# The second layer's norm gain moves into its weights: POOL scales the weight blocks, ACT applies the row factor

## The reference, cut to what matters

```python
for l in range(DEPTH):                      # DEPTH = 2
    h = rms_norm(x, pre_norm_g[l])          # y = x * rsqrt(mean(x*x) + EPS);  y * g
    proj = einsum('bsd,de->bse', h, w_in)   # w_in_ab in layer 0, w_in_c in layer 1
    ...                                     # mixers A and B (layer 0), C (layer 1), gates
    y = einsum('bse,ed->bsd', y, w_out)
    x = x + rms_norm(y, post_norm_g[l])
```

## Time and profile before

| | us |
|---|---|
| three executions | 1218.23, 1218.73, 1219.78 |
| the profiled execution | 1218.22 |
| its span | 1216.4 |
| TensorE busy (PE) | 1186.4 |
| DVE busy | 805.5 |
| ACT busy | 589.1 |
| POOL busy | 432.4 |

### The profile page before, as it was taken

One profiled execution on the slowest core, in us unless ns is written; L12 is line 12 of the kernel. 1 busy time (PEld: TensorE's weight loads), 2 busy tenths in 40 slices (PEclk: granted clock), 3 DMA queues, 4 the chain that ended last, 5 costly groups with the idle time before them and its releaser, 6 DMA issues.

```text
span 1216.4 us, 17708 instructions
## 1 busy us (share of the span) xinstructions
PE 1186.4 (98%) x6520; PEld 1011.3 (83%) x6520; DVE 805.5 (66%) x1710; ACT 589.1 (48%) x1296; POOL 432.4 (36%) x557
## 2 busy tenths in 40 slices
PE   9999999999999999898999999999999999999995
PEld 8988888888888887787788888888888888888874
DVE  5464765756667668867554866857658568485677
ACT  6554444434444556655454544544435444345464
POOL 5433214133163464646752214124141241222312
PEclk9999999999999999999999999999999999999998
DMA  6261101011031153235121102011020110201107
GB/s 200 71 188 47 59 18 52 19 52 35 19 87 53 53 156 105 70 114 156 65 78 51 50 19 74 18 57 53 18 74 19 57 53 19 73 19 31 44 20 136
DMA packets 93560, 78.42 MB, mean 64 GB/s; under 512 B 3074, under 2 KB 83970, under 8 KB 93475
## 3 DMA queue, kind: packets, MB, share of 16 engines
q1 hardware_dynamic: 92466, 73.63, 19.9%
q0 software_dynamic: 1008, 3.67, 1.8%
HBM read 68.85 MB, written 13.68 MB: 68 GB/s over the span
## 4 chain that ended last, share of the span: by engine, by line
PE 47%; DVE 2%; ACT 1%; POOL 1%; issue 1%; DVEq 0%; ACTq 0%; POOLq 0%
PE dense L1126 26%; PE dense L1137 7%; PE pv_ps L1259 6%; PE scores L1339 4%; PE turned L1306 4%; PE turned L1294 0%; DVE pT_lo L1844 0%; DVE fin L2040 0%; POOL w_lo L978 0%; ACT k_hh L1448 0%; DVE e_sb L1779 0%; POOL rowstat L1004 0%; POOL rowstat L1001 0%; DVE y L1763 0%; ACT junk L1630 0%
## 5 line engine op out<-in xcount | busy, mean ns | idle before, releaser
L1126 PE MATMUL dense<-hT_hi,w_hi 128*128 128x512 f32 x880 | 350.7, 399 | 0.0
L1126 PE MATMUL dense<-hT_lo,w_hi 128*128 128x512 f32 x880 | 344.7, 392 | 0.0
L1126 PE MATMUL dense<-hT_hi,w_lo 128*128 128x512 f32 x880 | 344.2, 391 | 0.0
L971 POOL TENSOR_SCALAR w_hi<-w_f 128x1024 fp32r<-128x1024 f32 x86 | 93.2, 1084 | 642.2 <-PE dense L1126 585.2
L978 POOL TENSOR_TENSOR w_lo<-w_f,w_hi 128x256 fp32r<-128x256 f32 x344 | 266.3, 806 | 7.2
L1455 ACT ACTIVATE e_sb<-e_sb,low 128x256 f32<-128x256 f32 (+7 forms) x256 | 170.3, 665 | 171.5 <-DVE low L1779 169.2
L1488 ACT ACTIVATE pT_hi<-turned 128x640 fp32r<-128x640 f32 (+3 forms) x224 | 117.2, 523 | 165.7 <-PE pv_ps L1259 95.2
L1126 PEld LDWEIGHTS dense<-hT_hi,w_lo 128*128 128x128 f32 x880 | 165.5, 188 | 36.8
L1126 PEld LDWEIGHTS dense<-hT_hi,w_hi 128*128 128x128 f32 x880 | 166.0, 189 | 26.1 <-issue 0.3
L1126 PEld LDWEIGHTS dense<-hT_lo,w_hi 128*128 128x128 f32 x880 | 166.2, 189 | 25.1
L1844 DVE TENSOR_TENSOR pT_lo<-turned,pT_hi 128x640 fp32r<-128x640 f32 (+3 forms) x224 | 133.6, 597 | 39.6 <-ACT pT_hi L1488 39.4
(11 more groups left out here) (213 smaller groups left out, 1804.4 us busy)
## 6 DMA issues: line engine op xcount, KB each, us to landing
w_f<-in_w_in_c SPq DMA_DIRECT2D x37, 512.0 KB, 4.2
w_f<-in_w_in_ab SPq DMA_DIRECT2D x34, 512.0 KB, 3.9
rel_tiles_dram<-rel_rows_dram SPq DMA_DIRECT2D x1, 5120.0 KB, 23.0
bias<-rel_tiles_dram SPq DMA_DIRECT2D x8, 640.0 KB, 5.4
y<-in_x SPq DMA_DIRECT2D x8, 512.0 KB, 7.7
hT_lo_f<-in_x SPq DMA_DIRECT2D x8, 512.0 KB, 7.3
out_x<-y SPq DMA_DIRECT2D x8, 512.0 KB, 3.6
w_f<-in_w_out_c SPq DMA_DIRECT2D x8, 512.0 KB, 3.8
```

The lines of the kernel that those rows point to most:

```text
L971: ts(hi, src, 1.0, 1.0, ALU.mult, ALU.mult).then_inc(w_hi_done, 1)
L1126: last = mm(dense[:, x.n % 2, :], lhs[:, d * P:(d + 1) * P], rhs[:, d, x.f * HALF:(x.f + 1) * HALF], start=i == 0, stop=i == 23)
```

## The change

The helper `takes_g` names 37 of the weight blocks: all of layer C's input projection. For these, POOL's `split` first waits for g_pre, multiplies each of the block's eight 128x128 tiles in place by a factor per partition (a column of g_pre), waits for these to be done, and then splits as before. SP loads g_pre's eight columns with eight small loads in place of one. The instruction that applied the row's root and g_pre on DVE is removed, and ACT applies the root alone, as a copy with a scale, behind the squares of its step.

```diff
+def takes_g(w):
+    return w.u.kind == "C" and w.b != "o"
...
-                sp.dma_start(g_pre[:], pre_norm_g[1].partition_broadcast(P)).then_inc(s_gpre, 16)
+                for d in range(DT):
+                    sp.dma_start(g_pre[:, d:d + 1], pre_norm_g[1][d * P:(d + 1) * P].rearrange("(p a) -> p a", a=1))\
+                        .then_inc(s_gpre, 16)
...
-        def split(n, hi_slot, slot, loads):
+        def split(n, hi_slot, slot, loads, scaled=0):
             if new(w_loaded[slot], 16 * loads):
                 pool.wait_ge(w_loaded[slot], 16 * loads)
-            src, hi = f32_place(slot), hi_place(hi_slot)
+            src, hi, lo = f32_place(slot), hi_place(hi_slot), lo_place(slot)
+            if scaled:
+                if new(s_gpre, 16 * DT):
+                    pool.wait_ge(s_gpre, 16 * DT)
+                for d in range(DT):
+                    part = (slice(None), d // 4, slice(d % 4 * P, (d % 4 + 1) * P))
+                    last = ts(src[part], src[part], g_pre[:, d:d + 1], None, ALU.mult)
+                last.then_inc(w_scaled, 1)
+                if new(w_scaled, scaled):
+                    pool.wait_ge(w_scaled, scaled)
             ts(hi, src, 1.0, 1.0, ALU.mult, ALU.mult).then_inc(w_hi_done, 1)
...
             for w in SPLITS_AT.get(s, []):
                 freed_by(w.hi_free)
-                split(PRO_SPLITS + w.n, w.hi, w.slot, w.loads)
+                split(PRO_SPLITS + w.n, w.hi, w.slot, w.loads,
+                      1 + sum(1 for o in WEIGHTS if o.n < w.n and takes_g(o)) if takes_g(w) else 0)
...
+            for n in NORM:
+                r = n.r
+                if s == n.scaled:
+                    if new(n_xr, r + 1):
+                        act.wait_ge(n_xr, r + 1)
+                    if new(n_sum, r + 1):
+                        act.wait_ge(n_sum, r + 1)
+                    copy(x_place(r), by_tile(y[:, r, :]), ACT.Copy, scale=rowstat[:, 5, r:r + 1]).then_inc(n_scaled, 1)
...
-            for n in NORM:
-                r = n.r
-                if s == n.scaled:
-                    if new(n_xr, r + 1):
-                        dve.wait_ge(n_xr, r + 1)
-                    if new(s_gpre, 16):
-                        dve.wait_ge(s_gpre, 16)
-                    if new(n_sum, r + 1):
-                        dve.wait_ge(n_sum, r + 1)
-                    stt(out=x_place(r), in0=by_tile(y[:, r, :]), scalar=rowstat[:, 5, r:r + 1], in1=by_tile(g_pre[:]),
-                        op0=ALU.mult, op1=ALU.mult).then_inc(n_scaled, 1)
```

More of the change, by code:

```diff
@@ L719, in program @@
     w_loaded = [sem(f"w_loaded{i}") for i in range(7)]
-    w_hi_done, w_ready = sem("w_hi_done"), sem("w_ready")
+    w_scaled, w_hi_done, w_ready = sem("w_scaled"), sem("w_hi_done"), sem("w_ready")
     s_filled, s_hi_out = sem("filled"), sem("hi_out")
@@ L973, in split @@
                 pool.wait_ge(w_hi_done, n + 1)
-            lo = lo_place(slot)
             for h in range(2):
```

## The result

| | before | after |
|---|---|---|
| median of the executions | 1218.48 (4) | 1267.20 (4), from 1266.44 to 1267.88 |
| ratio after / before | | 1.0398, 95% interval 1.038 to 1.0416 |
| the profiled execution, its span | 1218.22, 1216.4 | 1267.12, 1265.3 |
| mean granted clock of TensorE | 0.995 | 0.979 |

The median before now has a fourth execution, 1217.97. The forecast was 1218.3 in a range from 1216.2 to 1222.4. The change costs 4.0%, and the time lies far above the range.

What follows compares the result with a forecast made beforehand. TensorE, busy 98%, bounds the kernel; only its 9.4 us of waits for normalisation between the layers could be won. First rows -1.0 plus bridge +0.6 gave -0.4, a median of 1218.3 us, range 1216.2 to 1222.4.

Steps and rivals of the forecast that it cites:

- Part 1: Rows 0 to 3, normalised while units of kind B run: DVE relieved; -1.0 us, between 0 and -2.0.
- The price of a multiplication: POOL's added 128x128 multiplication by g_pre: 0.30 us each, 2.5 us per block, between 2.0 and 3.7.
- In the long stage of C ... nothing: Layer C's long stage: 2.5 us per split lie beside two fills, so they cost nothing.
- Part 2: Rows 4 to 7, bridge into layer C: 2.8 us won turn into waits; +0.6 us, between -0.6 and +3.
- The wait for v of C1: Bridge: the split of v ends at 584.95, TensorE gets there at 582.4 and must wait 2.5 us.
- (a): Bridge: scaled splits k, g, v end about 564.0, row 4's root behind them; its sum some 0.25 us late.
- the +0.6 of the sum: Bridge: TensorE turns row 6 at 586.95 where before it did at 586.35, +0.6 us.
- (d): Splits from 593 on, each waiting for TensorE to free the high part: slack 2.8 us against 2.5, barely holds.
- the dear rival: POOL's multiplications cost 0.45 us each, 3.7 per block, over the slack: +6.4, 1225; decides from 0.36 each; chance 0.20.
- The rule weighed: POOL and DVE contend for SBUF at 577 to 584 us; applying this would move the sum by 0.2.
- The clock: TensorE's new bridge waits, up to 3.9 us, lower its clock: 1.6 us lost, sum +1.2, 1220; chance 0.2.
- DVE was the only cause: Roots not delayed, multiplications cost 0.25: bridge -0.6, first rows -2.0, time 1216.1; chance 0.10.

Runs made afterwards that it cites:

- Experiment 8: Changed kernel, but DVE instead of ACT applies the row factor, as a one-input operation; POOL's scaling stays: 1268.14 us, ratio 1.0408.
- experiment 5: Changed kernel with constant 1.0 in place of g_pre in POOL's eight multiplications per block, product with g_pre left out: 1227.48 us, ratio 1.0072.
- experiment 2: Changed kernel with only four of each scaled block's eight tiles multiplied, the other half left out: 1229.92 us, ratio 1.0081.
- experiment 3: Changed kernel with the output weights' split ahead of the scaled split of v in five units of layer C: 1236.71 us, ratio 1.0141.
- experiment 1: Changed kernel with no block scaled, layer 1's product with g_pre left out, row factor still on ACT: 1215.83 us, ratio 0.997.
- experiments 6: Changed kernel with one wide two-input multiplication per block, g_pre's eight columns broadcast, in place of eight small ones: 1223.11 us, ratio 1.004.
- experiment 7: Changed kernel with one wide two-input multiplication per block, done before POOL waits for the free high part: 1222.07 us, ratio 1.0026.
- experiments 9: Kernel of experiment 7 with the block v of unit C1 multiplied by itself earlier, ahead of the bridge's roots: 1218.65 us, ratio 0.9999.
- 13: Kernel of experiment 9 with the row factor of rows 0 to 3 on DVE, rows 4 to 7 on ACT: 1218.57 us, ratio 1.0.
- 14: Kernel of experiment 13 with the output weights' split ahead of that of v in five units of layer C: 1218.22 us, ratio 0.9996.

## Why the prediction was wrong

By its own steps:

**Part 1 was right.** Forecast -1.0, measured -1.1 (508.88 to 507.75); the matmul behind the first wait stands 1.4 us sooner, as said (486.82 to 485.43). The 2.6 us wait at the first rows is down to 1.2, and the clock of 486.8 to 491 is 1.00 where it was 0.61. Experiment 8 adds that ACT is not needed for it: a shorter instruction on DVE wins 1.6. Why that is 0.5 more was not tested by itself; of the waits, the one for the factor itself is 1.3 us with ACT and 0.6 with DVE.

**The price of a multiplication failed: the first wrong step.** "I take 0.30 each, as the shape is the mask's", 2.5 per block, 3.7 at most. Measured: 0.60 median, 4.67 per block. The mask carries its factors in the instruction, the new form reads one per partition from SBUF, and experiment 5 shows that this is all of the difference. I had written that no row showed the form, and then set the upper bound by a guess (what doubling the columns costs) rather than by a row. A safe upper bound near by would have been the two-input operation, 0.71 us for 128x256, or 5.7 for eight.

**"In the long stage of C ... nothing" failed: the second wrong step.** 31.5 of the 48.9 us arise at its five places. I had read the slack only of the blocks that are scaled. The unscaled one behind v on POOL had 0.18 us, and 0.53 of idle time ahead of it. The two errors work on each other, so neither is the whole: at the assumed price (experiment 2) the time is 37.3 us less and this step still costs 8.2 us of waits; by order alone, at the true price (experiment 3), it is 30.5 us less. The 540 us window at 538.3 busy was read as "nothing to win", which is true; it says nothing about how near to losing each of its waits is.

**Part 2, the bridge: the right places, the sizes too small, mostly by the price.** The wait for v of C1 came, behind its split as described, and row 6 behind that; the forecast was 2.5 us for the wait and 586.95 for row 6, measured were 4.65 and 596.20. In (a) three scaled splits were to end at 564.0. They end at 570.71, 6.7 us late, and 3 x (4.75 - 2.5) = 6.75 says why (4.75 with the wait ahead of the split, as in the 2.5). That alone brought a wait of 5.94 us. With the assumed price, experiment 2, the wait at v of C1 was 2.4, but row 6 was turned 1.6 us late for the +0.6 of the sum, and 2.8 us of clock came on top, which the sum left to a rival. (d) failed as the dear rival said: 4.75 against 2.8 of slack, and a wait of 1.79.

**The rule weighed.** The Trainium skill, "GPSIMD Engine Reference", section "Engine selection", calls a one-input operation on GpSimd roughly line rate. Experiment 5 and the added form differ by a factor of two at one shape, so no single rate holds for one-input operations here; the form with a factor per partition belongs with the dear ones. Its advice, elementwise work on VectorE, is borne out by POOL's 0.60 us for 128x128 beside DVE's 0.75 for 128x1024 (experiment 8). The prediction gives the other rule, of "SBUF — State Buffer", section "Who interferes with whom", without its condition: the Trainium skill exempts a Vector instruction with one SBUF input only outside the two-port performance modes. No term of the sum hangs on it.

**The rivals.** *Dear multiplications* (0.20) is what happened, with its mechanism and its places in the bridge. Its threshold of 0.36 us each fits, without being tested closely: the splits behind 593 brought no wait at 2.5 per block (experiment 2) and one of 1.79 at 4.75. Its time, 1225, was too low by 42 us, since it took 3.7 per block and had the long stage at nothing. *The clock* (0.20) came true beside it. At the assumed price it costs 2.8 us, where the rival had 1.6. Waits far apart did not add up: the five of 1.6 us in experiment 2, some 80 us apart, left the clock at 1.00, while behind those of 4.06 it was 0.50 to 0.57. *DVE was the only cause* (0.10) holds for experiment 1 alone: 3.6 us below before, where the rival had 2.6; that 1215.83 lies so near its 1216.1 is in part luck, since before stood at 1219.42 in that group.

**The view that would have told.** For each split, the end of w_lo against the start of the first matmul that reads it: the lines at 750.44 and 755.46 of before, and the 0.53 us of idle time in the line at 749.31. A cost of 2.5 us against 0.7 us, five times, is 9 us: about 1227 in place of 1218.3, even at 0.30 us each. Experiment 2 measured 8.2 us in the five waits, and 1229.92 with what the clock and the bridge add.

## What to carry to other kernels

Before adding work to an engine that runs a fixed order, read the slack of everything queued behind it, the instructions the change doesn't touch included: end of the product against start of its first use. An engine that is idle two thirds of the time may have its idle time ahead of the new work and none behind it, and then the same work put before the wait costs a fraction (it took 38.5 of the 48.7 us away here). A price for a form of instruction that no row shows is not bounded by rows of the same shape; bound it by the dearest row near by, and give the chance that it decides accordingly.

## What the runs showed of the hardware beside that

- On POOL a 128x128 f32 operation with constant factors takes 0.304 us, with a factor per partition 0.618 (experiments 5 and after).
- POOL's two-input multiplication over 128x1024, its second input spread from eight columns, takes 1.92 us, where four subtractions of 128x256 take 2.77 to 2.83 together: the one large instruction is the cheaper here, though the operation and the second input differ too. Beside DVE the one for v of C1 took 2.75 (experiments 6 and 7).
- Beside that instruction DVE's two-input operation over 128x1024 took 2.09 to 2.57 us, where it took 1.22 without (experiments 9, 13, 14 and 1).
- The row factor over 128x1024 f32 takes 0.75 us on DVE with one input, 1.14 on ACT as a copy with a scale (the prediction had taken 1.06 from its square), and 1.28 and more on DVE with two inputs.
- The granted clock behind a wait of TensorE, as a mean over 4 to 8 us: 1.00 after 1.6 us (experiment 2), 1.00 after 2.4 (before, at 575), 0.77 after 1.9 with another of 1.2 close by (experiment 7), 0.65 after 2.4 with another of 1.2 (experiment 2), 0.50 to 0.57 after 4.06.
- One profiled execution against another of the same first 400 us differs by up to 1.8 us (450.33 to 452.14), nearly all of it from ahead of 85 us. A shift smaller than that has to be counted from a matmul ahead of the change.
